# Index products two panels earlier, lent panels in the first block alone, and another order in the experts' first iteration, in a two-block transformer kernel

## The reference

```python
def first_block(x, mem, ...):            # 2 layers
    # layer 0: moba attention + pooling ("mix0"); layer 1: spatial gating + delta rule ("mix1")
    # then in both: memory_cross_attention ("xat0", "xat1"), conv_ffn ("ffn0", "ffn1")
    ...
def memory_cross_attention(xn, mem_n, wq, wkv, wo):
    q = (xn @ wq); k, v = split(mem_n @ wkv)          # 4 heads of 256
    p = softmax(q k^T * 256 ** -0.5)
    return (p v) @ wo

def second_block(x, c, ada_w, ada_b, ...):   # 2 layers
    # mod = silu(c) @ ada_w[l] + ada_b[l]: six parts of 1024 per layer (shift, scale, gate, twice)
    # o_a, o_b, o_c, o_d: four attentions side by side, 4 heads each ("mix2", "mix3")
    #   a differential, b with latent queries and keys, c on keys chosen by index scores, d banded
    # layer 0: swiglu ("ffn2"); layer 1: 8 experts, two per token ("ffn3")
```

## Time and profile before

| what | value |
|---|---|
| device time, median of 3 | 2718.67 us (2716.99 to 2718.99) |
| the profiled execution | 2718.73 us, its span 2716.9 us |
| TensorE busy | 2624.9 us, 97% |
| VectorE, ScalarE, GpSimd busy | 1739.2, 1308.8 and 259.9 us |
| mean granted clock of TensorE | 0.987 of full speed |
| mean HBM rate | 231 GB/s |

### The profile page before, as it was taken

How to read it: one execution, slowest core, us unless ns; L and a number is a source line. 1 busy time by engine, 2 the same in 40 slices (tenths; PEclk the granted TensorE clock), 3 DMA queues, 4 the chain that set the end, 5 groups by cost and what they waited for, 6 DMA issues and landing times.

```text
span 2716.9 us, 39062 instructions
## 1 busy us (share of the span) xinstructions
PE 2624.9 (97%) x13682; PEld 2178.8 (80%) x13682; DVE 1739.2 (64%) x2543; ACT 1308.8 (48%) x1925; POOL 259.9 (10%) x248
## 2 busy tenths in 40 slices
PE   7999999998999999999999998999999999999998
PEld 6687999887678998767998775878787878787886
DVE  1212776562117773655554564989898989889897
ACT  2211544411015442243332242877777777777776
POOL 0141000640310004200004100000000000000000
PEclk9999999899999999999999998999999999999999
DMA  8254545441445446305455303989898989898897
GB/s 319 93 202 152 205 185 185 159 156 62 155 144 205 186 186 217 149 32 200 185 186 197 139 32 132 368 323 373 329 378 321 375 329 373 323 353 349 340 352 286
DMA packets 87634, 627.28 MB, mean 231 GB/s; under 512 B 9760, under 2 KB 9920, under 8 KB 12800
## 3 DMA queue, kind: packets, MB, share of 16 engines
q1 hardware_dynamic: 84512, 613.45, 59.8%
q0 software_dynamic: 2480, 11.31, 1.1%
q10 hardware_dynamic: 560, 1.38, 0.1%
HBM read 625.06 MB, written 1.05 MB: 230 GB/s over the span
## 4 chain that ended last, share of the span: by engine, by line
PE 92%; DVE 4%; ACT 2%; issue 1%; DMA 0%; DVEq 0%; SPq 0%; ACTq 0%
PE bank L947 22%; PE bank L838 14%; PE bank L975 11%; PE bank L601 11%; PE bank L852 7%; PE bank L790 6%; PE bank L614 6%; PE bank L688 2%; PE bank L1036 2%; PE bank L650 2%; PE bank L1075 1%; PE bank L990 1%; PE bank L917 1%; PE bank L962 1%; PE bank L674 1%
## 5 line engine op out<-in xcount | busy, mean ns | idle before, releaser
L1412 ACT ACTIVATE sb_parts<-sb_ring 128x1024 fp32r<-128x1024 f32 x873 | 873.4, 1052 | 168.0 <-PE bank L790 82.8
L2151 DVE TENSOR_TENSOR sb_parts<-sb_ring,sb_parts 128x1024 fp32r<-128x1024 f32 x675 | 786.3, 1217 | 6.6 <-ACT sb_parts L1412 6.6
L947 PE MATMUL bank<-sb_parts 128*128 128x512 f32 x2688 | 662.1, 396 | 8.4 <-DVE sb_parts L2151 5.7
L947 PEld LDWEIGHTS bank<-sb_parts 128*128 128x128 f32 x2688 | 495.6, 188 | 118.3 <-issue 9.7
L838 PEld LDWEIGHTS bank<-sb_parts 128*128 128x128 f32 x3168 | 385.4, 192 | 8.2 <-issue 6.1
L838 PE MATMUL bank<-sb_parts 128*128 128x256 f32 x3168 | 386.6, 284 | 5.5 <-DVE sb_XT L2076 4.2
L975 PE MATMUL bank<-sb_parts 128*128 128x512 f32 x1344 | 323.8, 390 | 0.0
L975 PEld LDWEIGHTS bank<-sb_parts 128*128 128x128 f32 x1344 | 251.7, 188 | 52.1
L601 PE MATMUL bank<-sb_XT,sb_ring 128*128 128x256 f32 x1152 | 261.6, 388 | 7.0 <-DVE sb_XT L1896 4.0
L601 PEld LDWEIGHTS bank<-sb_XT,sb_ring 128*128 128x128 f32 x1152 | 222.4, 195 | 42.9 <-issue 12.1
L2053 DVE TENSOR_TENSOR sb_parts<-sb_ring,sb_parts 128x1024 fp32r<-128x1024 f32 x198 | 232.7, 1219 | 24.4 <-ACT sb_parts L1412 24.4
(11 more groups left out here) (343 smaller groups left out, 2399.4 us busy)
## 6 DMA issues: line engine op xcount, KB each, us to landing
sb_ring<-in_moe_panels SPq DMA_DIRECT2D x342, 1024.0 KB, 6.2
sb_ring<-in_ada_w SPq DMA_DIRECT2D x48, 1024.0 KB, 4.9
sb_ring<-in_ffn_w_up SPq DMA_DIRECT2D x44, 1024.0 KB, 4.9
sb_ring<-in_ffn_w SPq DMA_DIRECT2D x33, 1024.0 KB, 4.9
sb_ring<-in_w_in SPq DMA_DIRECT2D x26, 1024.0 KB, 4.8
sb_ring<-in_ffn_w_down SPq DMA_DIRECT2D x22, 1024.0 KB, 7.2
sb_ring<-in_xattn_wkv SPq DMA_DIRECT2D x16, 1024.0 KB, 4.8
sb_ring<-in_od_w_in SPq DMA_DIRECT2D x12, 1024.0 KB, 4.9
```

The lines of the kernel that those rows point to most:

```text
L947: m = nc.tensor.matmul(banks[par][:, :], x[:, k, :], w[:, cols], start=k == 0 and t == 0, stop=k == KD - 1 and t == 2, skip_group_check=True)
L1412: return nc.scalar.activation(out, in_, ACT.Copy)
L2151: V_.tensor_tensor(LOW[u], ring[slot][:, 1024 * c:1024 * c + 1024], HIGH[u], ALU.subtract) \
```

## The change

There are three edits. (1) In mix2 and mix3 the four index products of the second token half move from behind a_v and c_q to behind a_q and a_k, with ScalarE's rectifying of them; c_q becomes a panel beside unit 0 of the attention, and the panels behind it shift. (2) No panel is lent in mix2 and mix3 any more. Two are lent in mix0, ahead of output panels 0 and 2, eight in xat0 (five before), eight in xat1 (four before); mix1 keeps its eight. The takes in the cross attentions are spread, one behind each panel or unit, by the table `TAKE_LATER`. (3) In an expert's first iteration VectorE makes the second low part of the next panel ahead of `hidden`.

```diff
-        LENT_AHEAD = {"xat0": (("xq", 0, 0), ("xq", 0, 2), ("xk", 0, 0), ("xv", 0, 0), ("xv", 0, 2)),
+        LENT_AHEAD = {"mix0": (("out", "mix0", 0), ("out", "mix0", 2)),
+                      "xat0": tuple(("xq", 0, j) for j in range(4)) + (("xk", 0, 0), ("xk", 0, 1), ("xv", 0, 1), ("xv", 0, 3)),
...
-                      "xat1": (("xq", 1, 0), ("xq", 1, 2), ("xv", 1, 0), ("xv", 1, 2)),
-                      "mix2": tuple(("s0", x) for x in ("b_qd", "a_q", "a_v", "c_k", "d_q")),
-                      "mix3": tuple(("s1", x) for x in ("b_qd", "a_q", "a_v", "c_k"))}
+                      "xat1": tuple(("xq", 1, j) for j in range(4)) + tuple(("xv", 1, j) for j in range(4))}
+        TAKE_LATER = {"xat0": {("xq", 1): (2, 4), ("xq", 3): (1, 5), ("xk", 0): (1, 6), ("xk", 1): (1, 7),
+                               0: (1, 7), 1: (1, 6), 2: (1, 7), 5: (1, 6), 6: (1, 7)},
...
-        LATE = {0: "c_k", 1: "c_v", 3: "d_q", 4: "d_k", 6: "d_v"}
+        LATE = {0: "c_q", 1: "c_k", 3: "c_v", 4: "d_q", 5: "d_k", 6: "d_v"}
...
-                    if key[0] == "x" and s == 5:
-                        take((f"xat{key[1]}", 1), 2, 7)
-                        if key[1] == "0":
-                            take((f"xat{key[1]}", 2), 1, 6)
+                    if key[0] == "x" and s in TAKE_LATER[f"xat{key[1]}"]:
+                        take((f"xat{key[1]}", s), *TAKE_LATER[f"xat{key[1]}"][s])
...
                 panel_T((k2, "a_q"))
+                for j in range(2):
+                    index_scores(1, j)
                 panel_T((k2, "a_k"))
+                for j in range(2, 4):
+                    index_scores(1, j)
...
                 panel_tok((k2, "a_v"))
-                for j in range(2):
-                    index_scores(1, j)
-                panel_T((k2, "c_q"))
-                take((n, 0), 2, 5)
-                for j in range(2, 4):
-                    index_scores(1, j)
-
...
                 evac((k2, "a_q"), QA)
+                rectified(1, (0, 1))
                 evac((k2, "a_k"), KA)
+                rectified(1, (2, 3))
...
                 evac((k2, "a_v"), VA)
-                rectified(1, (0, 1))
-                evac((k2, "c_q"), QC)
-                rectified(1, (2, 3))
...
-                def step_(E, it, i=0):
+                def step_(E, it, i=0, first=False):
 
                     low(E, "low_k", it + 1, 0, i)
+                    if first:
+                        low(E, "low_k", it + 1, 1, i)
                     hidden(E, it, i)
-                    low(E, "low_k", it + 1, 1, i)
+                    if not first:
+                        low(E, "low_k", it + 1, 1, i)
```

More of the change, by code:

```diff
@@ L497, in build_program @@
                   "ffn2": 3, "mix3": 3, "ffn3": 2}
-        LENT_AHEAD = {"xat0": (("xq", 0, 0), ("xq", 0, 2), ("xk", 0, 0), ("xv", 0, 0), ("xv", 0, 2)),
+        LENT_AHEAD = {"mix0": (("out", "mix0", 0), ("out", "mix0", 2)),
+                      "xat0": tuple(("xq", 0, j) for j in range(4)) + (("xk", 0, 0), ("xk", 0, 1), ("xv", 0, 1), ("xv", 0, 3)),
                       "mix1": (("qkv", 0), ("qkv", 2), ("qkv", 4), ("u", 0), ("u", 1), ("vz", 0), ("vz", 1), ("gate", 0)),
-                      "xat1": (("xq", 1, 0), ("xq", 1, 2), ("xv", 1, 0), ("xv", 1, 2)),
-                      "mix2": tuple(("s0", x) for x in ("b_qd", "a_q", "a_v", "c_k", "d_q")),
-                      "mix3": tuple(("s1", x) for x in ("b_qd", "a_q", "a_v", "c_k"))}
+                      "xat1": tuple(("xq", 1, j) for j in range(4)) + tuple(("xv", 1, j) for j in range(4))}
+        TAKE_LATER = {"xat0": {("xq", 1): (2, 4), ("xq", 3): (1, 5), ("xk", 0): (1, 6), ("xk", 1): (1, 7),
+                               0: (1, 7), 1: (1, 6), 2: (1, 7), 5: (1, 6), 6: (1, 7)},
+                      "xat1": {("xq", 2): (1, 4), ("xq", 3): (1, 5), 0: (1, 7), 1: (1, 6), 2: (1, 7), 3: (1, 6),
+                               5: (1, 7), 6: (1, 6)}}
         LENT_TO = {name: stage for stage, names in LENT_AHEAD.items() for name in names}
@@ L744, in late @@
                         panel_T(name, bank=bank)
[L745 to L748, removed]
                 if s == TURN_AT:
@@ L784, in project @@
                         wait_read(*needs[pair])
+                    if ("out", name, rp) in LENT_TO:
+                        lend(LENT_TO["out", name, rp])
                     n, slot = panel()
@@ L804, in cross @@
                 normed(n)
[L805 to L809, removed]
+                for x, j in [("xq", j) for j in range(4)] + [("xk", j) for j in KEYS_FIRST[layer]]:
+                    panel_T((x, layer, j), rhs=XT if x == "xq" else MT)
+                    if (x, j) in TAKE_LATER[n]:
+                        take((n, x, j), *TAKE_LATER[n][x, j])
                 wait_read(*[(x, layer, j) for x in ("xq", "xk") for j in range(4)])
@@ L1500, in late @@
                 if s in LATE:
-                    evac((key, LATE[s]), {"c_k": KC, "c_v": VC, "d_q": QE, "d_k": KE, "d_v": VE}[LATE[s]])
+                    evac((key, LATE[s]), {"c_q": QC, "c_k": KC, "c_v": VC, "d_q": QE, "d_k": KE, "d_v": VE}[LATE[s]])
                 if s == TURN_AT:
@@ L1938, in attention @@
                         late(key, s, layer)
+                    if key[0] == "x" and s < 4 and s in TAKE_LATER[f"xat{key[1]}"]:
+                        taken((f"xat{key[1]}", s))
                     if s in BESIDE.get(key, {}):
@@ L1995, in late @@
                     m.then_inc(sem("rope_done"), 1)
-                if s == 5:
-                    taken((f"mix{2 + layer}", 1))
                 if s == BIAS_AT:
@@ L2008, in late @@
                     step(m)
-                if s == 7 and layer == 0:
-                    taken((f"mix{2 + layer}", 2))
                 if s == TURN_AT:
@@ L2035, in cross @@
             def cross(layer, n):
[L2036 to L2040, removed]
+                for x, j in [("xq", j) for j in range(4)] + [("xk", j) for j in KEYS_FIRST[layer]]:
+                    if j % 2:
+                        evac((x, layer, j), (QT if x == "xq" else KT)[:, 2 * j:2 * j + 2, :])
+                    if (x, j) in TAKE_LATER[n]:
+                        taken((n, x, j))
                 attention(f"x{layer}")
-                taken((n, 1))
-                if layer == 0:
-                    taken((n, 2))
+                for t in (5, 6):
+                    taken((n, t))
                 add_sum(n)
@@ L2212, in experts @@
                         added(E)
-                        step_(E, 0)
+                        step_(E, 0, first=True)
                         dve.wait_ge(full[7], E * BANK_FILLS[7] + (base[7] + 2))
@@ L2690, in _ @@
             pool.wait_ge(sem("silu_cond"), 1)
+            sum_lent("mix0")
             sum_lent("xat0")
@@ L2713, in _ @@
                               .broadcast_to([P, KD, 4, 32])).then_inc(sem("ki_spread"), 1)
-                sum_lent(f"mix{2 + layer}")
             pool.wait_ge(sem("residual_ready"), COUNTED.index("mix3") + 1)
```

1 line of the change is left out of this document (removed).

## The result

The changed kernel takes 2723.65 us (median of 11 runs, 2719.89 to 2733.43), the kernel before took 2716.99 us beside it (11 runs, 2715.98 to 2720.16). The ratio is 1.0028, 95% interval 1.0020 to 1.0037: slower by 0.3%, where I had forecast 2714.5 us and at most 2719.5. The profiled execution of the changed kernel took 2728.47 us (span 2726.6, 9.7 more than before), so it is one of its longer ones.

The account below looks back on a forecast made before the run. TensorE bounds the kernel, with 92% of the span. Terms -3.0 (mix2) -2.2 (mix3) -5.5 (experts) +3.0 (xat0) +1.2 (last takes) +1.3 (mix0) +1.0 (clock) = -4.2 from 2718.73: 2714.5 us, range 2709.5 to 2719.5.

Parts of the forecast that it names:

- The clock term: Lower TensorE clock behind two new waits of about 2 us, each with chance one half: +1.0 us, bounds 0 to 3.2.
- c_q at nothing: Panel c_q, moved beside unit 0 in mix2 and mix3, costs nothing but its own 7 us, spent before too.
- The 3.4 us at the up-projection: Wait at the latents' second product (line 737) falls from 3.94 to 0.5 us: minus 3.4 per layer, mix2 and mix3.
- the 2.1 before a_v: New TensorE wait ahead of panel a_v in mix2 and mix3, for ScalarE's rectifying: +2.1 us each, bounds 1.2 to 2.7.
- rival 4: Wait at line 737 stays as VectorE enters unit 0 later; if in full, 11.0 us return: 2725.5 us, chance 0.06.
- the overlap in mix3: At mix3's unit 0, a 0.7 us wait for a_v's copy plus 1.0 of lost overlap with index products: +1.7 us.
- go with the idle time they follow: Half-clock stretches behind the line 737 wait vanish with it: minus 1.6 us in mix2, minus 2.6 in mix3.
- Experts, -5.5: Eight 0.71 us waits in the experts' first iterations vanish: -5.5 us, bounds -3 to -5.7.
- xat0, +3.6: First cross attention: waits of 1.8 and 1.2 us for panels xk 0 and xk 1, plus 0.6 for the last take.
- xat1: Second cross attention: panels at least 5 us ahead, so 0 for panel waits; its last take costs 0.6 us.
- mix0, +1.3: GpSimd's two lent-panel sums slow VectorE's scalings in mix0's last units: +1.3 us, bounds 0.3 to 3.4.
- rival 3: First block eats the gain: xat1 starves like xat0 (+3.0) and the clock falls once (+1.6): 2719 us, chance 0.19.

Follow-up runs that it names:

- the move and the sums first: VectorE's second-half index sums ahead of its latent copy: in the changed kernel 2716.11 us; in the kernel before with move and experts' edit 2706.91, plus bank turn by two 2702.45.
- the turn's run: Changed kernel with the turn of the four banks moved on by one behind a_v, where c_q used to take one: 2723.17 us, ratio 1.0016.

## Why the prediction was wrong

**The clock term failed.** "Two new waits of that size, each with a chance of one half, would be 1.6; as they are a little shorter I take +1.0, bounds 0 and 3.2". That is the step that failed, by its size and with the sign of the result: behind the two waits before a_v the clock cost 1.7 and 3.0, 4.7 us, in both profiles of the changed kernel, and with the waits it went (a_v took 7.1 us in both layers of all three kernels that have the move and the sums first). Five profiles have these waits (the changed kernel twice, without the experts' edit, with the turn, the move alone): behind 9 of the 10 waits the clock was at its lower level within a_v, not in mix2 of the move alone. The price of a stretch was taken as 1.6, half of a short one; the one in mix3 is twice as long in three of the five profiles, and TensorE works through 6.1 of its 6.8 us. Over the ten waits it comes to 1.9 us each. Another 1.6 us stood behind the panel's wait in xat0 in the first profile (that panel takes 8.73 us), where I had allowed nothing. And I weighed a chance of one half from one wait of 2.2 us in each layer, two cases.

**A term was missing: ffn2, +2.5.** I had c_q at nothing, since it stands "where TensorE was busy and VectorE had time". But a claim that leaves the turn shifts every later claim, and the wait at the start of ffn2 grew by 1.63 us; the turn's run shows that. The rest is a stretch of half clock that is 6.8 us long instead of 3.4. It is not shown to come from the longer wait: all four profiles with the wait of 5.9 us have it, but so have three of the eight with the wait of 4.2, and there the stage took 206.0 us instead of 204.7. So the bank is worth 1.2 to 1.6 us and the stretch 1.3.

**The second block otherwise.** The 3.4 us at the up-projection were measured as 3.66 in each layer and the 2.1 before a_v as 2.08, so mix2 and mix3 hold in their waits. The cause that I gave was the wrong one, or half of it: "ScalarE is late because VectorE is", yes, but VectorE was late by GpSimd's sums, which the lent panels' part removes alone. I had the row (four steps in 4.37 us) and used it only against rival 4. Had each edit been priced alone, the move would have stood at +4.2 for waits, +1.7 for the overlap in mix3 and the clock, with no gain left to it. At mix3's entry, 17 us behind its norm's start, there is another stretch of half clock, 1.6 us for a panel that takes 8.73, in every profile of a kernel with an edit in the second block, and none in the two of before and that of the experts' edit. What sets it off stays open; it was 6.8 us long in three of the ten profiles that have it. And a stretch that goes can come back elsewhere: the 2.2 us wait at line 755 is the same in mix3 of all 13 profiles, and half clock stands behind it in seven, which are just those without a stretch of 6.8 us at a_v or at the up-projection before it. I had let the stretches "go with the idle time they follow".

**Experts, -5.5**: 5.3 in the profiles of the changed kernel and of the edit alone, 6.1 in the medians. The step holds.

**xat0, +3.6**: waits for panels of 2.2 and 0 in one profile, 1.9 and 1.2 in the other, against 1.8 and 1.2; the last take 0.56 against 0.6. What was left out is the bank wait ahead of the first scores, 0.86 and 0.70 us for VectorE's sum of the take just made where 0.41 and 0.21 were, +0.45 in xat0 and +0.5 in xat1, and the clock. **xat1** needed 0 for panels, as said.

**mix0, +1.3**: 1.1 and 2.2; the higher one has the stretch of half clock at its end, as have three other profiles. The pair that GpSimd hits in full takes 2.32 us, longer than the 1.81 of the earlier trace rows, the next 0.98:

```profile
103.01 2.32 DVE L1931 TENSOR_SCALAR sb_REG<-sb_REG,sb_small 128x256 f32<-128x256 f32 x2
```

By the Trainium skill (SBUF — State Buffer, Who interferes with whom) a VectorE instruction in a two-port mode fully blocks while a GpSimd instruction that came first holds the shared pair. The trace does not show in which mode the scalings ran. For two of them I had reckoned 2.3 us more by that rule (twice the row's 1.0 us are 2.0, two of the 1.27 us instructions that ran here 2.5) and had taken 1.2; it is 1.7 here, between the two. The tail as a whole stayed by the forecast.

**mix1 and the router** were given 0. mix1 differs by 4.9 us between two executions of the same kernel, by the length of one stretch; it is no part of the change. Between the starts of the router's norm and of the experts' panels the first profile lost another 3.3 us to half clock (from 11.7 us behind to 15.0), and won 5.3 after. How much of this the change sets off, the runs do not settle. Of the 11 runs of the changed kernel, those at a mean clock of 0.983 and 0.984 took 2724.8 us or more of span, those at 0.986 to 0.988 at most 2721.9.

Summed against the forecast: clock behind a_v +3.7, xat0's panels with their clock +0.1 to +0.8, ffn2 +2.5, mix3's entry +1.6, bank waits ahead of the scores +1.0 give 8.9 to 9.6 of the 10.9 us between -4.2 and the +6.7 of the medians. The rest is not placed; it is less than what mix1 alone differs by between two executions. None of the rivals had this: rival 3 comes nearest in time, but xat1 never waited for a panel, and the wait of rival 4 went as forecast.

## What to carry to other kernels

Where two edits of one change remove the same wait, price each alone with the other already made: the second may buy nothing and still bring its own waits. An operation that leaves a rotating allocation shifts everything that is allocated behind it, so look where the next stage's first claim lands. The waits of 2.1 us ahead of a long panel had in 9 cases of 10 a stretch of half clock behind them, which cost 1.9 us on average over the ten; and before moving work up on one engine, see that its consumer is not queued behind something that comes later.

## What the runs showed of the hardware

- The same kernel's longest stretch of half clock (mix1) was 23.9 and 10.2 us in two executions, and 13.7 and 17.1 for the kernel before; the stage then took 252.9 and 248.0, 250.7 and 252.3 us. Stage lengths from one profile each tell differences of a few us only where the stretches of half clock are the same.
- GpSimd's sums slow VectorE beyond its scalings: the add of two 128x256 tiles took 1.38 us beside them and 0.42 alone, a 128x1 add 1.11 against 0.16.
- Which part of the norm held the bank of the first product of ffn2 set its wait: 5.9 us for the fourth, 4.2 for the third, 2.3 for the first. In the stage's length that is 1.2 us for the first step and about 0.7 for the other, with the stretch of half clock equally long.
